# Expert jobs of a two-block transformer kernel: bias row a job ahead, scatter split in two, halves copied in another order

## Chip, cores and metric

The kernel runs on one core of a Trainium2 chip. The metric is the device time of one execution in microseconds; 2043.29 us is the median of three runs (2041.34 to 2046.06).

## The reference

A first block and a second block of two layers work on 256 tokens of width 1024, all in float32. The change touches one part of the first block: a mixture of 32 experts, of which each token uses 4.

```
def moe_ffn(h, w_router, b_router, w1, b1, w2, b2):
    logits = (hf @ w_router + b_router).astype(jnp.float32)
    top_val, top_idx = lax.top_k(logits, TOP_K)          # TOP_K = 4
    gates = jax.nn.softmax(top_val, axis=-1)
    ...
    def expert_block(args):
        xb, e = args
        hh = xb @ w1[e] + b1[e]                          # w1[e]: 1024 x 2048
        return swiglu_clamped(hh) @ w2[e] + b2[e]        # w2[e]: 1024 x 1024
```

The clamped SwiGLU takes the even columns of `hh` as `glu` (clamped above at 7) and the odd ones as `lin` (clamped to -7 .. 7) and gives `glu * sigmoid(1.702 * glu) * (lin + 1)`. The results are weighted with the gates and added up per token.

## The kernel before

A list of jobs is made on the chip once the router is done. A job is one expert with up to 64 of its tokens; an expert with more tokens gets a second job. Jobs are run two by two in a hardware loop on TensorE, ScalarE and VectorE each (`Fori(0, turns)`, r = 0 and 1 in each turn), and the engines meet only at semaphores.

Weights come through a ring of twelve buffers of 1 MB. SyncE issues the transfers (L405): an expert is twelve chunks, eight of w1 (chunks 0 to 7, one for each 128 rows) and four of w2 (8 to 11). Chunk j of the next expert may be issued when chunk j of the last job of the present expert has been used (`job_chunk`, counted up by TensorE behind each chunk).

One job on TensorE (`expert`, L800 to L842), in the order of its queue:

- w1 (L811): eight chunks, four matmuls each. The 64 tokens are the stationary operand; the two halves of the 2048 columns go to partitions 0 to 63 and 64 to 127 of banks 4 and 5.
- bias (L818): four matmuls with one row each, which add b1 as the last step of the sum; `hidden` tells VectorE.
- scatter (L792): eight matmuls that add the previous job's y, weighted with its gates, to the output in banks 0 to 3. It needs the previous y (L1382) and gate matrix (L1364).
- gather (L776): three of four blocks of tokens for the next pair of jobs; then the four transposes of the activation (L828), the last block of the gather, two transposes of gates (L782).
- w2 (L840): four chunks into bank 7, once ScalarE has copied the transposed activation (L1374).

In the profile each float32 matmul is two MATMUL instructions, so w1 has 64 of them, the bias 8, the scatter 16, w2 32.

VectorE in a job (L1843 to L1855): build index masks; wait for `hidden`; clamp glu (L1849) and lin (L1850) out of PSUM, each reading every second value of 1024; (lin + 1) * glu (L1853); wait for the sigmoid; the product (L1855), which is written in the order that the transposes want, as w2's rows lie in pairs: consecutive values go to places 128 values apart. ScalarE in a job (L1366 to L1382): issue the transfer of this job's b1 row (L1369), sigmoid (L1372), copy of the transposed activation (L1374), copies of gathered tokens and gates, copy of y (L1382).

"The middle" of a job below is the stretch from the last w1 matmul to the first w2 matmul.

Of the kernel before, what the change touches and what calls it, by code (L numbers as in the profile page):

```python
# [10 lines left out]
ALU = mybir.AluOpType  # L11
# [4 lines left out]
P = 128  # L16
D = 1024
T = 256
KT = D // P
# [15 lines left out]
E_N = 32  # L35
# [4 lines left out]
LISTED = 64  # L40
LIMIT = 7.0
# [15 lines left out]
CHUNK = 2048  # L57
N_ADA_A, N_WIN, N_ADA_B, N_WOUT = 8, 12, 16, 4
PER_EXPERT = 12
C_ADA_A = 0  # L60
C_WIN = C_ADA_A + N_ADA_A
C_ADA_B = C_WIN + N_WIN
# [111 lines left out]
sub_sq sub_ssq sub_root mix_ready dve_step   # L174
logits_ready top_ready e_ready masks_ready ranks_ready gates_ready gates_turned gates_saved tok_turned tok_saved
count_ready 
masks_built picks_built gathered half_saved xg_ready st_saved hidden hidden_read glu_ready sig_ready act_ready act_turned act_saved
y_saved pass_over b1_even b1_odd jobs_listed jobs_turned
moe_step job_chunk
rot_ready ret_v_ready ret_scores ret_weighted ret_out ret_sq ret_ssq ret_root  # L180
# [21 lines left out]
def two_layer_program(nc, x, c, w_ada, b_ada, g_pre_mix, g_post_mix, w_in, w_out, lam_q1, lam_k1, lam_q2,  # L202
# [4 lines left out]
    with ExitStack() as ctx:  # L207
# [3 lines left out]
        S = namedtuple("Semaphores", NAMES)(*[ctx.enter_context(nc.semaphore(n)) for n in NAMES])  # L211
# [11 lines left out]
        jobs = sbuf("jobs", 2 * LISTED + 2 + E_N, I32, rows=1)  # L223
        psum = ctx.enter_context(nc.psum_tensor("psum", [P, 8 * 512], F32))
        bank = [psum[:, 512 * i:512 * i + 512] for i in range(8)]
# [59 lines left out]
        pick = region(4608, TT * 2 * SLOTS).rearrange("p (a s) -> p a s", a=TT)  # L285
        pick_g = [region(4864 + 256 * i, TT * 2 * SLOTS).rearrange("p (a s) -> p a s", a=TT) for i in range(2)]
        glu, lin, sig, act_rows = (region(5376 + 512 * i, 512) for i in range(4))
        hidden_pairs = [t.rearrange("p (q m k) -> p q m k", q=2, k=2) for t in (lin, sig)]
        act_pairs = act_rows.rearrange("p (q k m) -> p q m k", q=2, k=2)
        b1_rows = [v[:, 0:1024].rearrange("p (h n) -> p h n", h=2) for v in (mixT, sq)]  # L290
        pos = region(15140, TT * (PASSES * E_N + 2)).rearrange("p (a e) -> p a e", a=TT)
        gate = region(9028, TT * 34).rearrange("p (a e) -> p a e", a=TT)
# [189 lines left out]
        def _(pe):  # L482
# [263 lines left out]
            for q in range(4):  # L746
                mm = routed_part(q)
# [34 lines left out]
                    mm = nc.tensor.transpose(home[:, a * P:(a + 1) * P], pick_g[r][:, a, :], ident)  # L782
                mm.then_inc(S.gathered, 1)

            def scatter(r, before, last=False):

                pe.wait_ge(S.y_saved, before + 1)
                pe.wait_ge(S.st_saved, before + 1)
                for t in range(4):
                    for h in range(2):  # L790
                        k, half = 4 * h + t, slice(64 * h, 64 * h + 64)
                        mm = nc.tensor.matmul(bank[k // 2][:, (k % 2) * T:(k % 2 + 1) * T],  # L792
                                              y_sb[half, t * P:(t + 1) * P], st_sb[r][half, :], start=False, stop=last,
                                              skip_group_check=True)
                return mm
# [4 lines left out]
            def expert(pair, r):  # L800
                e = pair * 2 + r
                weights = pe.value_load(jobs[0:1, bass.ds(pair * 2 + (LISTED + r), 1)], min_val=0, max_val=E_N - 1)
                if r == 0:
                    pe.wait_ge(S.xg_ready, pair + 1)
                pe.wait_ge(S.hidden_read, e + 1)
                pe.wait_ge(S.st_saved, e + 1)
                for k in range(KT):
                    chunk_here(weights, k)
                    for q in range(2):
                        for h in range(2):  # L810
                            mm = nc.tensor.matmul(bank[4 + q][64 * h:64 * h + 64, :], xg[:, k, SLOTS * r:SLOTS * (r + 1)],  # L811
                                                  ring[(C_MOE + k) % RING][:, (2 * h + q) * 512:(2 * h + q + 1) * 512],
                                                  start=(k == 0), stop=False)
                    mm.then_inc(S.job_chunk, 1)
                pe.wait_ge((S.b1_even, S.b1_odd)[r], pair * 16 + 16)
                for q in range(2):
                    for h in range(2):
                        mm = nc.tensor.matmul(bank[4 + q][64 * h:64 * h + 64, :], ones[64 * q:64 * q + 1, 0:64],  # L818
                                              b1_rows[r][64 * q:64 * q + 1, h, :], start=False, stop=True)
                mm.then_inc(S.hidden, 1)  # L820
                scatter(1 - r, e)
                if r == 0:
                    pe.wait_ge(S.picks_built, pair + 2)
                pe.wait_ge(S.half_saved, e + 2)
                gather(range(4 * r, 4 * r + 3), bank[6])
                pe.wait_ge(S.act_ready, e + 1)
                for t in range(4):
                    mm = nc.tensor.transpose(bank[4][:, t * P:(t + 1) * P], act_rows[:, t * P:(t + 1) * P], ident)  # L828
                mm.then_inc(S.act_turned, 1)
                gather((4 * r + 3,), bank[6])  # L830
                turn_gates(1 - r, e + 2, bank[5])
                pe.wait_ge(S.act_saved, e + 1)
                for j in range(8, 12):
                    chunk_here(weights, j)
                    w = ring[(C_MOE + j) % RING][:, :].rearrange("p (k n) -> p k n", k=2)
                    for k in range(2):
                        f = 2 * (j - 8) + k
                        at = (f % 4) * P + (f // 4) * 64
                        for h in range(2):
                            mm = nc.tensor.matmul(bank[7][64 * h:64 * h + 64, :], act_T[:, at:at + 64],  # L840
                                                  w[:, k, 512 * h:512 * h + 512], start=(f == 0), stop=(f == 7))
                    mm.then_inc(S.job_chunk, 1)  # L842
# [400 lines left out]
        def _(act):  # L1243
# [25 lines left out]
            at = KT  # L1269
# [95 lines left out]

            def expert(pair, r):  # L1366
                e = pair * 2 + r
                weights = act.value_load(jobs[0:1, bass.ds(pair * 2 + (LISTED + r), 1)], min_val=0, max_val=E_N - 1)
                act.dma_start(b1_rows[r][0:P:64], b1[0][bass.ds(weights, 1), :].rearrange("a (h q n) -> (a q) h n", h=2, q=2)) \  # L1369
                   .then_inc((S.b1_even, S.b1_odd)[r], 16)  # L1370
                act.wait_ge(S.glu_ready, e + 1)
                nc.scalar.activation(sig, glu, ACT.Sigmoid, scale=ALPHA).then_inc(S.sig_ready, 1)  # L1372
                act.wait_ge(S.act_turned, e + 1)
                nc.scalar.activation(act_T, bank[4], ACT.Copy).then_inc(S.act_saved, 1)  # L1374
                act.wait_ge(S.gathered, e + 2)
                save_half(r, bank[6], (xg_stage, xg[:, 4:8, :])[r])
                save_gates(1 - r, bank[5])
                if r == 1:
                    act.wait_ge(S.half_saved, e + 3)
                    nc.scalar.activation(xg[:, 0:4, :], xg_stage, ACT.Copy).then_inc(S.xg_ready, 1)  # L1380
                act.wait_ge(S.job_chunk, e * PER_EXPERT + PER_EXPERT)
                nc.scalar.activation(y_sb, bank[7], ACT.Copy).then_inc(S.y_saved, 1)  # L1382

            nc.scalar.activation(spare[:, 0:1], eps6, ACT.Copy).then_inc(S.y_saved, 1)
            act.wait_ge(S.count_ready, 1)
            turns = act.value_load(jobs[0:1, 2 * LISTED:2 * LISTED + 1], min_val=E_N // 2, max_val=E_N // 2 + 8)
            act.wait_ge(S.gathered, 1)
# [4 lines left out]
            with act.Fori(0, turns) as i:  # L1392
                for r in range(2):
                    expert(i, r)
            act.wait_ge(S.pass_over, 1)
            for q in range(4):
                square(psum, q)
# [196 lines left out]
        def _(dve):  # L1594
# [243 lines left out]
            with dve.Fori(0, turns) as i:  # L1838
                moe_chain.turn = i * 2
                for r in range(2):  # L1840
                    e = i * 2 + r

                    if r == 0:  # L1843
                        dve.wait_ge(S.gathered, e + 1)
                        pick_pair(lambda n: place_at(i * 2 + (n + 2)))
                    pick_gates(1 - r, place_at(i * 2 + (r + 1)), column_at(i * 2 + (r + 1)))
                    dve.wait_ge(S.hidden, e + 1)
                    both = psum[:, 4 * 512:6 * 512].rearrange("p (f g) -> p f g", g=2)
                    V.tensor_scalar(glu, both[:, :, 0], LIMIT, None, ALU.min).then_inc(S.glu_ready, 1)  # L1849
                    V.tensor_scalar(lin, both[:, :, 1], LIMIT, -LIMIT, ALU.min, ALU.max).then_inc(S.hidden_read, 1)  # L1850
                    dve.wait_ge(S.glu_ready, e + 1)
                    dve.wait_ge(S.hidden_read, e + 2)
                    moe_chain.link(V.scalar_tensor_tensor(out=lin, in0=lin, scalar=1.0, in1=glu, op0=ALU.add, op1=ALU.mult))  # L1853
                    dve.wait_ge(S.sig_ready, e + 1)
                    V.tensor_tensor(act_pairs, hidden_pairs[0], hidden_pairs[1], ALU.mult).then_inc(S.act_ready, 1)  # L1855
            onto_x(3, psum, 8, lambda q: only_gained(q, 88, gained_4))
            inverse(4)
            gained(88)
# [264 lines left out]
```

## Time and profile before

| | |
|---|---|
| median of 3 runs | 2043.29 us (2041.34 to 2046.06) |
| profiled execution | span 2042.2 us; the page gives no other time for it |
| TensorE busy | 1971.6 us (97%) |
| VectorE, ScalarE busy | 457.9 us (22%), 332.7 us (16%) |
| DMA | 562.30 MB, mean 275 GB/s; the expert weights are 384 transfers of 1 MB |
| chain that ended last | PE 79%, DMA 14%, SyncE's queue 4% |
| w1 matmuls (L811) | 2176 instructions, 491.0 us busy; 39.9 us idle ahead of them, nearly all for transfers |
| expert loop | first w1 matmul at 245.25 us, last y copy ends at 1207.4 us |

The page divides the span into 40 slices of 51 us. A matmul's duration is from its start to its modelled end, and matmuls overlap, so the time that one adds is read from the distance between starts.

### The profile page before, as it was taken

The numbers are of one execution on the slowest core, as the hardware profiler recorded it, in microseconds if no ns is written. First come the engines' busy times: TensorE is split into PE (matmuls) and PEld (weight loads), VectorE is DVE, ScalarE is ACT, GpSimd is POOL, SyncE is SP. The second block draws the span as 40 slices with busy tenths as digits, with TensorE's granted clock in tenths as the row PEclk, the third lists the DMA queues.
The fourth block names the chain that finished last, engine by engine and source line by source line (L and its number), as shares of the span: only waits on it lengthen the run. The fifth ranks groups of instructions, "written<-read, shape, count | busy, mean of one in ns | idle before, by whom it ended". The sixth has DMA issues, their size and how long they took to land.

```text
span 2042.2 us, 25651 instructions
## 1 busy us (share of the span) xinstructions
PE 1971.6 (97%) x10181; PEld 1262.8 (62%) x10182; DVE 457.9 (22%) x877; ACT 332.7 (16%) x689; POOL 19.1 (1%) x33
## 2 busy tenths in 40 slices
PE   7999999999999999999999989999999999999998
PEld 4876644433334444443333338788888899888887
DVE  1441311110111111111101122541010377410102
ACT  1232211111111111111111123431000121210001
POOL 2000000000000000000000000000000000000000
PEclk8999799999999999999999999999999999999999
DMA  9839299999999979999999996234445433344410
GB/s 350 284 120 405 85 422 421 422 422 422 421 383 373 422 314 421 422 421 421 422 421 422 422 367 202 92 124 141 148 149 160 140 108 104 124 144 153 157 42 21
DMA packets 170137, 562.30 MB, mean 275 GB/s; under 512 B 10486, under 2 KB 110104, under 8 KB 117600
## 3 DMA queue, kind: packets, MB, share of 16 engines
q1 hardware_dynamic: 167648, 554.96, 69.9%
q0 software_dynamic: 1664, 5.77, 1.0%
q8 instruction: 45, 0.74, 0.1%
q10 hardware_dynamic: 768, 0.74, 0.1%
q14 instruction: 12, 0.10, 0.0%
HBM read 560.38 MB, written 1.05 MB: 275 GB/s over the span
## 4 chain that ended last, share of the span: by engine, by line
PE 79%; DMA 14%; SPq 4%; DVE 1%; issue 1%; ACT 0%; DVEq 0%
PE psum L1106 15%; PE psum L811 14%; DMA ring<-in_w_dram 13%; PE psum L840 8%; PE psum L1078 7%; PE psum L1139 5%; PE psum L885 5%; SPq L405 4%; PE psum L654 4%; PE psum L570 3%; PE psum L776 3%; PE psum L792 2%; PE psum L1160 1%; PE psum L818 1%; PE psum L547 1%; DMA ring<-in_w_ada_dram 1%
## 5 line engine op out<-in xcount | busy, mean ns | idle before, releaser
L811 PE MATMUL psum<-ring,arena 128*64 128x512 f32 x2176 | 491.0, 596 | 39.9 <-DMA ring<-in_w_dram 39.7
L811 PEld LDWEIGHTS psum<-ring,arena 128*64 128x64 f32 x2176 | 152.3, 137 | 372.8 <-issue 252.9
L1106 PE MATMUL psum<-hT,ring 128*128 128x256 f32 x1408 | 307.5, 379 | 0.0
L1106 PEld LDWEIGHTS psum<-hT,ring 128*128 128x128 f32 x1408 | 267.5, 190 | 36.4
L840 PE MATMUL psum<-ring,arena 128*64 128x512 f32 x1088 | 241.0, 595 | 3.3
L1849 DVE TENSOR_SCALAR arena<-psum 128x512 f32<-128x512 f32 x34 | 23.5, 692 | 734.7 <-PE psum L818 734.7
L840 PEld LDWEIGHTS psum<-ring,arena 128*64 128x64 f32 x1088 | 77.7, 137 | 144.8 <-issue 144.8
L1078 PE MATMUL psum<-arena,ring 128*128 128x256 f32 x640 | 141.4, 379 | 0.0
L1078 PEld LDWEIGHTS psum<-arena,ring 128*128 128x128 f32 x640 | 121.6, 190 | 16.5
L1372 ACT ACTIVATE arena<-arena 128x512 f32<-128x512 f32 x34 | 21.4, 630 | 513.3 <-DVE arena L1849 513.3
L776 PE MATMUL psum<-arena 128*128 128x128 f32 x576 | 81.7, 288 | 0.0
L776 PEld LDWEIGHTS psum<-arena 128*128 128x128 f32 x576 | 72.2, 198 | 11.9 <-issue 11.9
L1139 PE MATMUL psum<-hT,ring 128*128 128x256 f32 x352 | 79.1, 379 | 0.0
L1534 ACT ACTIVATE arena<-arena 128x512 f32<-128x512 f32 x22 | 13.8, 629 | 394.5 <-DVE arena L1990 394.5
L792 PEld LDWEIGHTS psum<-arena 64*128 64x128 f32 x560 | 51.2, 186 | 33.8 <-issue 27.6
L1139 PEld LDWEIGHTS psum<-hT,ring 128*128 128x128 f32 x352 | 65.8, 190 | 10.1 <-issue 1.9
L792 PE MATMUL psum<-arena 64*128 64x256 f32 x560 | 69.9, 389 | 0.7 <-ACT arena L1382 0.7
L1990 DVE TENSOR_TENSOR arena<-psum,rstd 128x512 f32<-128x512 f32 x22 | 15.2, 692 | 238.3 <-PE psum L1106 238.3
L885 PE MATMUL psum<-hT,ring 128*128 128x256 f32 x288 | 66.3, 384 | 0.0
L570 PE MATMUL psum<-mixT,ring 128*128 128x256 f32 x288 | 63.9, 380 | 0.0
L654 PE MATMUL psum<-hT,ring 128*128 128x256 f32 x256 | 60.6, 394 | 0.5 <-DVE hT L1664 0.5
L885 PEld LDWEIGHTS psum<-hT,ring 128*128 128x128 f32 x288 | 53.8, 191 | 9.3 <-issue 2.4
(357 smaller groups left out, 1627.9 us busy)
## 6 DMA issues: line engine op xcount, KB each, us to landing
ring<-in_w_dram SPq DMA_DIRECT2D x384, 1024.0 KB, 22.8
ring<-in_ffn_w_dram SPq DMA_DIRECT2D x66, 1024.0 KB, 5.1
ring<-in_w_ada_dram SPq DMA_DIRECT2D x24, 1024.0 KB, 11.0
ring<-in_odd_w_in_dram SPq DMA_DIRECT2D x16, 1024.0 KB, 5.5
ring<-in_even_w_in_dram SPq DMA_DIRECT2D x13, 1024.0 KB, 12.7
ring<-in_w_in_dram SPq DMA_DIRECT2D x12, 1024.0 KB, 15.5
ring<-in_w_out_dram SPq DMA_DIRECT2D x4, 1024.0 KB, 15.6
ring<-in_even_w_out_dram SPq DMA_DIRECT2D x4, 1024.0 KB, 5.2
```

Source lines behind the costliest of these rows:

```text
L405: sp.dma_start(home[:, :], src).then_inc(landed[(C_MOE + j) % RING], 16)
L570: mm = nc.tensor.matmul(home[:, at:at + n_out], lhs, rhs, start=(k == 0), stop=(k == KT - 1))
L654: mm = nc.tensor.matmul(home, lhs, rhs, start=(k == 0), stop=(k == KT - 1))
L776: nc.tensor.matmul(home[:, (k % 4) * P:(k % 4 + 1) * P], h_tok[:, a, k * P:(k + 1) * P], pick[:, a, :], start=(a == 0), stop=(a == TT - 1))
L792: mm = nc.tensor.matmul(bank[k // 2][:, (k % 2) * T:(k % 2 + 1) * T], y_sb[half, t * P:(t + 1) * P], st_sb[r][half, :], start=False, stop= ...
L811: mm = nc.tensor.matmul(bank[4 + q][64 * h:64 * h + 64, :], xg[:, k, SLOTS * r:SLOTS * (r + 1)], ring[(C_MOE + k) % RING][:, (2 * h + q) * ...
L840: mm = nc.tensor.matmul(bank[7][64 * h:64 * h + 64, :], act_T[:, at:at + 64], w[:, k, 512 * h:512 * h + 512], start=(f == 0), stop=(f == 7))
L885: mm = nc.tensor.matmul(home[:, at:at + n_out], lhs, rhs, start=(k == 0), stop=(k == KT - 1))
L1078: mm = nc.tensor.matmul(bank[j // 2][:, (j % 2) * T:(j % 2 + 1) * T], w[:, k, j * P:(j + 1) * P], ffn_h[i % 2][:, k, :], start=(i == 0 and ...
L1106: mm = nc.tensor.matmul(bank[4 + 2 * (i % 2) + b][:, h * T:(h + 1) * T], cols(n)[:, k, h * P:(h + 1) * P], hT[:, k * T:(k + 1) * T], start ...
L1139: mm = nc.tensor.matmul(home, lhs, rhs, start=(k == 0), stop=(k == KT - 1))
L1849: V.tensor_scalar(glu, both[:, :, 0], LIMIT, None, ALU.min).then_inc(S.glu_ready, 1)
```

## The change

- **Bias.** ScalarE issues the transfer of the b1 row one job ahead (`load_b1` for the other buffer), and once ahead of the loop for expert 0. TensorE waits for the row and runs the four bias matmuls before w1, with `start=True`; the last w1 chunk ends the sum. The semaphore `hidden` is gone, VectorE waits for the eighth chunk of the job instead. Behind the loop ScalarE waits for the one row that was fetched in vain.
- **Scatter.** Its first half (t = 0, 1) runs behind w1's chunk 4 (k == SCATTER_AFTER), its second half (t = 2, 3) behind chunk 7, where all of it was.
- **Halves.** VectorE reads glu and lin with a step of four values, 256 of one parity and then 256 of the other, so that its results already lie in transposing order, and the product is written in order. The place of each block in the transposed activation changes with it (`at`).

```
-            def scatter(r, before, last=False):
+            def scatter(r, before, parts=range(4), last=False):
...
-                for t in range(4):
+                for t in parts:
...
+                pe.wait_ge((S.b1_even, S.b1_odd)[r], pair * 16 + 16)
+                for q in range(2):
+                    for h in range(2):
+                        nc.tensor.matmul(bank[4 + q][64 * h:64 * h + 64, :], ones[64 * q:64 * q + 1, 0:64],
+                                         b1_rows[r][64 * q:64 * q + 1, h, :], start=True, stop=False)
                 for k in range(KT):
                     chunk_here(weights, k)
...
-                                                  start=(k == 0), stop=False)
+                                                  start=False, stop=(k == KT - 1))
                     mm.then_inc(S.job_chunk, 1)
-                pe.wait_ge((S.b1_even, S.b1_odd)[r], pair * 16 + 16)
-                for q in range(2):
-                    for h in range(2):
-                        mm = nc.tensor.matmul(bank[4 + q][64 * h:64 * h + 64, :], ones[64 * q:64 * q + 1, 0:64],
-                                              b1_rows[r][64 * q:64 * q + 1, h, :], start=False, stop=True)
-                mm.then_inc(S.hidden, 1)
-                scatter(1 - r, e)
+                    if k == SCATTER_AFTER:
+                        scatter(1 - r, e, range(2))
+                scatter(1 - r, e, range(2, 4))
...
-                        at = (f % 4) * P + (f // 4) * 64
+                        at = (2 * k + j % 2) * P + (f // 4) * 64
...
-                weights = act.value_load(jobs[0:1, bass.ds(pair * 2 + (LISTED + r), 1)], min_val=0, max_val=E_N - 1)
-                act.dma_start(b1_rows[r][0:P:64], b1[0][bass.ds(weights, 1), :].rearrange("a (h q n) -> (a q) h n", h=2, q=2)) \
-                   .then_inc((S.b1_even, S.b1_odd)[r], 16)
+                following = act.value_load(jobs[0:1, bass.ds(pair * 2 + (LISTED + r + 1), 1)], min_val=0, max_val=E_N - 1)
+                load_b1(1 - r, b1[0][bass.ds(following, 1), :])
...
+            load_b1(0, b1[0][0:1, :])
             act.wait_ge(S.count_ready, 1)
...
+            act.wait_ge(S.b1_even, turns * 16 + 16)
             act.wait_ge(S.pass_over, 1)
...
-                    dve.wait_ge(S.hidden, e + 1)
-                    both = psum[:, 4 * 512:6 * 512].rearrange("p (f g) -> p f g", g=2)
-                    V.tensor_scalar(glu, both[:, :, 0], LIMIT, None, ALU.min).then_inc(S.glu_ready, 1)
-                    V.tensor_scalar(lin, both[:, :, 1], LIMIT, -LIMIT, ALU.min, ALU.max).then_inc(S.hidden_read, 1)
+                    dve.wait_ge(S.job_chunk, e * PER_EXPERT + KT)
+                    V.tensor_scalar(glu_rows, hidden_rows[:, 0], LIMIT, None, ALU.min).then_inc(S.glu_ready, 1)
+                    V.tensor_scalar(lin_rows, hidden_rows[:, 1], LIMIT, -LIMIT, ALU.min, ALU.max).then_inc(S.hidden_read, 1)
...
-                    V.tensor_tensor(act_pairs, hidden_pairs[0], hidden_pairs[1], ALU.mult).then_inc(S.act_ready, 1)
+                    V.tensor_tensor(act_rows, lin, sig, ALU.mult).then_inc(S.act_ready, 1)
```

with `hidden_rows = psum[:, 2048:3072].rearrange("p (n k g) -> p g k n", k=2, g=2)` and `glu_rows`, `lin_rows` the two buffers as `"p (k n) -> p k n"`.

## Rows read from the trace of the kernel before

**Rows 1.** The page's slices, line of GB/s moved by the DMA engines.
```profile
GB/s 350 284 120 405 85 422 421 422 422 422 421 383 373 422 314 421 422 421 421 422 421 422 422 367 202 92 124 141 148 149 160 140 108 104 124 144 153 157 42 21
```

**Rows 2.** Chain that ended last, 560 to 640 us: start us, us, what.
```profile
572.16 27.84 DMA ring<-in_w_dram
600.04 1.94 PE psum L811 x8
```

**Rows 3.** Timeline of VectorE, L1849: start us, us, engine, what [idle before <- releaser].
```profile
423.69 0.69 DVE L1849 TENSOR_SCALAR arena<-psum 128x512 f32<-128x512 f32 x1 [21.06 <-PE psum L818]
453.51 0.69 DVE L1849 TENSOR_SCALAR arena<-psum 128x512 f32<-128x512 f32 x1 [25.57 <-PE psum L818]
...
603.07 0.69 DVE L1849 TENSOR_SCALAR arena<-psum 128x512 f32<-128x512 f32 x1 [21.23 <-PE psum L818]
629.64 0.69 DVE L1849 TENSOR_SCALAR arena<-psum 128x512 f32<-128x512 f32 x1 [22.33 <-PE psum L818]
```

**Rows 4.** Windows: length, busy us by engine, clock, DMA share, GB/s.
```profile
609.00:616.00 7.00, 7.00 (x36) 2.44 (x34) 0.00 (x0) 0.69 (x2) 0.00 (x0) 1.00 0.01 2
...
739.00:750.00 11.00, 10.90 (x57) 4.54 (x58) 1.55 (x7) 3.13 (x8) 0.00 (x0) 1.00 0.01 3
```

**Rows 5.** Timeline, SyncE's queue, at the loop's start and behind both pauses.
```profile
247.38 12.33 SPq L405 DMA_DIRECT2D ring<-in_w_dram  x8
...
616.73 0.34 SPq L405 DMA_DIRECT2D ring<-in_w_dram  x1
...
749.58 0.34 SPq L405 DMA_DIRECT2D ring<-in_w_dram  x1
```

**Rows 6.** Timeline of one job, TensorE, VectorE and ScalarE.
```profile
641.22 13.91 PE L811 MATMUL psum<-ring,arena 128*64 128x512 f32 x64
641.43 0.60 ACT L1382 ACTIVATE arena<-psum 128x512 f32<-128x512 f32 x1 [5.25 <-PE psum L840]
642.70 1.01 ACTq L1369 DMA_DIRECT2D mixT<-in_b_dram  x1
...
655.06 1.09 PE L818 MATMUL psum<-mixT,early_sb 1*64 1x512 f32 x8
656.07 2.00 PE L792 MATMUL psum<-arena 64*128 64x256 f32 x16
656.21 0.69 DVE L1849 TENSOR_SCALAR arena<-psum 128x512 f32<-128x512 f32 x1 [17.80 <-PE psum L818]
...
658.00 1.60 PE L776 MATMUL psum<-arena 128*128 128x128 f32 x12
658.33 1.07 DVE L1855 TENSOR_TENSOR arena<-arena 128x512 f32<-128x512 f32 x1
...
660.87 7.09 PE L840 MATMUL psum<-ring,arena 128*64 128x512 f32 x32
```

**Rows 7.** Timeline, TensorE's weight loads, same job.
```profile
655.05 0.21 PEld L818 LDWEIGHTS psum<-mixT,early_sb 1*64 1x64 f32 x8 [0.81 <-issue]
656.07 1.60 PEld L792 LDWEIGHTS psum<-arena 64*128 64x128 f32 x16 [0.81 <-issue]
...
667.36 0.15 PEld L811 LDWEIGHTS psum<-ring,arena 128*64 128x64 f32 x2 [0.28 <-issue]
```

**Rows 8.** Groups by line and form, VectorE: count, busy us, mean ns, idle before.
```profile
L1855 DVE TENSOR_TENSOR arena<-arena 128x512 f32<-128x512 f32 x34 | 36.5, 1072 | 1.2
...
L1849 DVE TENSOR_SCALAR arena<-psum 128x512 f32<-128x512 f32 x34 | 23.5, 692 | 734.7 <-PE psum L818 734.7
...
L1994 DVE TENSOR_TENSOR arena<-arena 128x512 f32<-128x512 f32 x22 | 15.2, 692 | 0.7
...
L1990 DVE TENSOR_TENSOR arena<-psum,rstd 128x512 f32<-128x512 f32 x22 | 15.2, 692 | 238.3 <-PE psum L1106 238.3
```

**Rows 9.** Timeline, the next stage's first transfers and its first matmul.
```profile
1178.89 46.49 SPq L375 DMA_DIRECT2D ring<-in_even_w_in_dram  x10
...
1218.35 1.10 PE L885 MATMUL psum<-arena,ring 128*128 128x256 f32 x4 [0.18 <-DVE arena L1605]
```

More of the change, by code:

```diff
@@ L59 @@
 PER_EXPERT = 12
+SCATTER_AFTER = 4
 C_ADA_A = 0
@@ L176 @@
 count_ready
-masks_built picks_built gathered half_saved xg_ready st_saved hidden hidden_read glu_ready sig_ready act_ready act_turned act_saved
+masks_built picks_built gathered half_saved xg_ready st_saved hidden_read glu_ready sig_ready act_ready act_turned act_saved
 y_saved pass_over b1_even b1_odd jobs_listed jobs_turned
@@ L287, in two_layer_program @@
         glu, lin, sig, act_rows = (region(5376 + 512 * i, 512) for i in range(4))
-        hidden_pairs = [t.rearrange("p (q m k) -> p q m k", q=2, k=2) for t in (lin, sig)]
-        act_pairs = act_rows.rearrange("p (q k m) -> p q m k", q=2, k=2)
+        hidden_rows = psum[:, 2048:3072].rearrange("p (n k g) -> p g k n", k=2, g=2)
+        glu_rows, lin_rows = (t.rearrange("p (k n) -> p k n", k=2) for t in (glu, lin))
         b1_rows = [v[:, 0:1024].rearrange("p (h n) -> p h n", h=2) for v in (mixT, sq)]
@@ L1382, in expert, with load_b1 @@
                 nc.scalar.activation(y_sb, bank[7], ACT.Copy).then_inc(S.y_saved, 1)
+            def load_b1(r, row):
+                act.dma_start(b1_rows[r][0:P:64], row.rearrange("a (h q n) -> (a q) h n", h=2, q=2)) \
+                   .then_inc((S.b1_even, S.b1_odd)[r], 16)
             nc.scalar.activation(spare[:, 0:1], eps6, ACT.Copy).then_inc(S.y_saved, 1)
+            load_b1(0, b1[0][0:1, :])
             act.wait_ge(S.count_ready, 1)
```

## The prediction

> **What bounds the kernel now.** I read the slices first [rows 1]. TensorE is busy nearly everywhere (97% of the span by the page), but from the sixth slice to the twenty-third, the expert loop, the rate of the DMA engines is flat, 421 or 422 GB/s in all but three. There are two full resources, and busy shares don't say which one counts. The chain of waits [rows 2] says which of the two ends last. Up to 600.04 us it is the weight transfer, and each new expert costs twelve chunks of it: VectorE's first read of a job comes 29.82 us after the one before (423.69, 453.51), 2.49 us a chunk [rows 3]. From 600.04 us it is TensorE alone, and the same mark comes every 26.57 us (603.07, 629.64). So a job is worth 26.6 us of TensorE or 29.8 us of transfer.
>
> Why do the two change places? 34 jobs (L1849's count, [rows 8]) serve 32 experts. An expert with a second job keeps its twelve chunks in the ring, and SyncE can fetch nothing until the second job frees them. In 609 to 616 and in 739 to 750 us the DMA share is 0.01 [rows 4], and the next transfers are issued at 616.73 and 749.58 us [rows 5], when the second job has finished its first chunk. The same happens at the start of the loop: the first new transfer goes out at 247.38 us, once the first job has done one chunk. After each restart the transfers run without a hole, so every microsecond by which a restart comes later stays in the loop, until something after the last transfer gives it back. The path is therefore:
> (a) first job's start to its first chunk's end (TensorE), then transfers until the chunk w1-7 of the job that reads at 603.07;
> (b) from there TensorE: the middle of that job, its w2, and the first chunk of the next job (616.73);
> (c) 616.73 to 749.58 = 132.85 us = 5 periods of 26.57, TensorE;
> (d) transfers again until w1-7 of the last job;
> (e) TensorE: middle and w2 of the last job, and all that follows.
> On this path there are therefore seven middles (one in b, five in c, one in e), seven job starts (a, b, five in c) and five passes over chunks 4 and 5 of w1 (c). In the other jobs the transfers run without a hole beside TensorE; where it waits for them it has 29.82 - 26.57 = 3.25 us of cover a job.
>
> **The change, part by part.** One TensorE-bound job is in [rows 6]. It starts at 641.22, the next one 26.57 later, at 667.79. Its w1 is 64 instructions, two every 0.429 us (its weight loads: 0.15 us and 0.28 idle, [rows 7]), so 32 x 0.429 = 13.73 us, to 654.95. The middle goes from there to 660.87, 5.92 us, and w2 takes the last 6.92.
>
> *The middle, g.* Now: bias from 655.06, VectorE starts at 656.21 (0.06 after the modelled end of the bias, 656.15), ends the product at 658.33 + 1.07 = 659.40, w2 starts at 660.87. TensorE is not idle there: scatter 656.07 to 658.00, so 0.121 us for each of its sixteen, then the gather's twelve at the same pace, 1.45 us, to 659.45. Both engines are ready for the transposes at the same moment, so speeding up one of them alone would bring nothing. After: VectorE waits for w1-7 itself, whose matmuls end at 641.22 + 13.91 = 655.13, so it starts at about 655.19, 1.02 us earlier. Its product writes in order instead of by a step of 128 values: 1072 ns (L1855, [rows 8]) becomes the 692 ns of the same form at L1994, 0.38 less. TensorE's own queue then has half the scatter, 0.97, and the gather, 1.45: ready 2.4 us after the last chunk, VectorE after 0.24 + (659.40 - 656.21) - 0.38 = 3.05. VectorE is last, and the middle is 5.92 - 1.02 - 0.38 = 4.52. g = -1.40 us. What is late next: TensorE now idles 0.6 us in the hole that the scatter used to fill.
>
> *The bias at the start, b.* Its eight instructions are not gone, they stand before w1. The boundary between w2 and the next w1 has no gap today (L811's weight loads follow L840's with the usual 0.28 us idle, [rows 7]), so they are paid in full: 655.06 to 656.07 is 1.01 us, and 0.11 for the change of shape ahead of it: b = +1.12. Bounds: 0.86 from two slots of 0.43 us with nothing for the changes of shape, 1.15 with one more 0.14. The prefetch itself costs nothing: the same one 8 KB issue a job on ScalarE's queue (1.0 us, at its old place behind the y copy [rows 6]), needed 26 us later instead of 13; one more issue stands before the loop, where ScalarE only waits for the router. ScalarE's new wait behind the loop is for a transfer issued at the last job's start, some 30 us before.
>
> *Half of the scatter after chunk 4, s.* Eight of sixteen instructions leave the middle (counted above) and stand in a w1 that had no hole in (c). 1.93 us / 2 = 0.97, and again entering and leaving another shape: s = +1.12; bounds 0.86 (four slots of half of 0.43) and 1.25. Its waits are met: y is saved at 641.43 + 0.60 = 642.03, the scatter would be asked for at about 651. What is queued behind it, chunks 5 to 7, shifts by s.
>
> *Reading the halves from PSUM.* VectorE takes every fourth value instead of every second. Bounds: 692 as now, or the 1072 of L1855, whose stepping is the only slow one in the loop. I take 692: the step of two already costs no more than the step of one (L1849 against L1990, both 692, [rows 8]). The higher end is a rival.
>
> A change of shape shows in TensorE's weight loads: inside w1 they stand idle for 0.28 us between pairs, before the bias and before the scatter for 0.81 [rows 7], as none is loaded ahead there. The old order has four such changes a job, the new one seven. Without them b and s would be at their low bounds, which is rival 2. A rule of the Trainium skill stands behind this, and it speaks against the inserted pieces: by "TensorEngine Tiling (Array Packing)", Key Properties, another tiling mode, unlike another tile of the same mode, makes TensorE drain first. The trace agrees.
>
> **The sum.** 7b + 5s + 7g = 7.84 + 5.60 - 9.80 = **+3.6 us**. In steps: restart (a) +1.12; (b) -1.40 + 1.12, so +0.84 at the first pause's end; (c) five periods of 26.57 + 0.84 = 27.41, so +5.04 at the second; (d) nothing, because 27.41 is still under 29.82; (e) -1.40. Behind the loop TensorE goes on as before: at 1218.35 it starts on the next stage's first chunk after 0.18 us of waiting for VectorE, and that stage's chunks are issued from 1178.89 on [rows 9], so the shift is carried to the end. Why a shorter middle doesn't pay: only seven of 34 lie on the path, and there TensorE was full already, so what leaves the middle is paid elsewhere.
> With b and s low, g as it is: 6.02 + 4.30 - 9.80 = +0.5. With both high and g = -1.35: 8.05 + 6.25 - 9.45 = +4.9. The profiled span is 2042.2 us (the page gives no other time for it), which makes 2045.8; the median of the three runs is 2043.29, 1.1 higher, and 2046.9 on that footing. The runs spread over 4.7 us.
>
> **Rivals.**
> 1. *The wide step in PSUM is slow.* Both reads at L1849 and L1850 cost 0.38 more, in a row, before the third operation; g = -1.40 + 0.76 = -0.64, the period 28.2. Time: 7.84 + 5.60 - 4.48 = +9.0, 2052.3 us. It decides as soon as the two reads are over 750 ns. For it: L1855 shows that a step can cost half as much again. Against it: 692 at step two. The Trainium skill, "SBUF — State Buffer", Specifications (TRN2), has a rule that points to this rival: PSUM is read in lines of 8 bytes, and each access that crosses into a new line pays. By that rule the step of two, where each value lies in a line of its own, would pay already, and the row shows that it does not; for step four no run here has a number.
> 2. *Inserted work slips in cheaply.* The bias and the half scatter use parts of the array side by side, and if the changes of shape cost nothing at their new places we are at +0.5: 2043.8 us. For it: the pieces are short. Against: idle weight loads at each such change.
> 3. *The product stays slow*, because its two inputs and not its output pattern make 1072 ns. Then g = -1.02 and the sum is +6.3: 2049.6. Against it: L1994 has two inputs in SBUF as well and takes 692.
> 4. *Faster.* Bias, scatter and gather fill the middle up to 659.45, and of the 1.42 us behind that at most 0.4 is a wait for ScalarE's copy of the activation (an estimate, from 0.60 for the y copy of the same size less what is queued beside it). Even a perfect filling gives five times 0.4 and 1.4 at the tail, -3.4: 2039.9. Nothing in the diff takes work off TensorE.
>
> **Chances.** Forecast 0.70 with its own range 2044 to 2049; rival 1 0.12; rival 2 0.10; rival 3 0.04; rival 4 0.04. What can be told from no change is about 0.2%, 4.1 us, and the forecast stands just inside: of its 0.70 I put 0.27 above the line, 0.42 within, 0.01 below. Slower 0.27 + 0.12 + 0.04 = 0.43; same 0.42 + 0.10 = 0.52; faster 0.05. The range of eight in ten goes from the low end of rival 2 less a microsecond of spread, 2042.7, to 2051, which leaves out most of rival 1.
>
> **What the changed profile would show.** The VectorE mark every 27.4 us between the two pauses (it was 26.57), 29.8 to 30.0 elsewhere. DMA restarts later than before against the first job's start by 1.1, 0.8 and 5.0 us. From the last w1 matmul's issue to w2 4.5 us. L1855's successor at 692 ns, the two reads at 692. TensorE's weight loads idle before and after the inserted half scatter. From the last job's w1-7 to the end 1.4 us less. The stretch bound by TensorE after the second pause lasts longer, since only 2.4 us instead of 3.3 of the lead are used up in each job. I am wrong if the period is under 26.6 (then b or s is hidden), if it is over 28 (the reads), or if the time moves outside the expert loop.

## The result, and the profile after

| | before | changed |
|---|---|---|
| median of 20 runs each | 2042.33 us (2039.03 to 2046.52) | 2045.53 us (2042.89 to 2050.67) |
| ratio | | 1.0020, 95% interval 1.0014 to 1.0026: +2.9 to +5.3 us |
| span of the profiled run | 2042.2 us | 2042.7 us |
| period between the two pauses | 26.57 us | 27.54 us |
| first job's start to the first matmul of the next stage | 973.10 us | 978.64 us |

The forecast was +3.6 us. The change costs about 0.2%; the interval starts at 0.14%, so it is clear of no change. The two spans differ by only 0.5 us because the profiled run of the changed kernel reached its first job 4.8 us earlier (240.42 against 245.25). That moment wanders: over the traces of all kernels below it lies between 240.4 and 245.5 us, and for the changed kernel itself at 240.42 and 243.36. So from here on traces are compared from the first job's start. Its first matmul and the next stage's first (as [rows 9]) are:

```profile
240.42 1.09 PE L811 MATMUL psum<-mixT,early_sb 1*64 1x512 f32 x8 [0.16 <-issue]
...
1219.06 1.10 PE L887 MATMUL psum<-arena,ring 128*128 128x256 f32 x4 [0.18 <-DVE arena L1612]
```

The wait of 0.18 us in front of the next stage is the one of before; all that was lost was lost in the loop.

The timeline of VectorE, first read of a job (as [rows 3]), in the changed kernel:

```profile
599.32 0.69 DVE L1855 TENSOR_SCALAR arena<-psum 128x512 f32<-128x512 f32 x1 [21.64 <-PE psum L817]
626.86 0.69 DVE L1855 TENSOR_SCALAR arena<-psum 128x512 f32<-128x512 f32 x1 [23.30 <-PE psum L817]
```

27.54 us where it was 26.57. The timeline of a job (as [rows 6]; its w1 began at 666.71 - 27.54 = 639.17) shows of what this is made:

```profile
647.91 1.13 PE L793 MATMUL psum<-arena 64*128 64x256 f32 x8
648.97 5.37 PE L817 MATMUL psum<-ring,arena 128*64 128x512 f32 x24
654.27 1.13 PE L793 MATMUL psum<-arena 64*128 64x256 f32 x8
654.39 0.69 DVE L1855 TENSOR_SCALAR arena<-psum 128x512 f32<-128x512 f32 x1 [19.14 <-PE psum L817]
...
655.34 1.60 PE L777 MATMUL psum<-arena 128*128 128x128 f32 x12
...
656.51 0.69 DVE L1861 TENSOR_TENSOR arena<-arena 128x512 f32<-128x512 f32 x1
657.25 0.66 PE L830 MATMUL psum<-early_sb,arena 128*128 128x128 f32 x4 [0.31 <-DVE arena L1861]
...
658.67 7.09 PE L842 MATMUL psum<-ring,arena 128*64 128x512 f32 x32
...
665.69 1.09 PE L811 MATMUL psum<-sq,early_sb 1*64 1x512 f32 x8
666.71 5.80 PE L817 MATMUL psum<-ring,arena 128*64 128x512 f32 x26
```

Five chunks take 8.58 us and end at 647.75; w1 goes on at 648.97, so s = 1.22. The other three end at 654.12, w2 starts at 658.67: the middle is 4.55, g = -1.37. The rest of 27.54 (less 13.73 of w1 and 6.92 of w2) is b = 1.12. TensorE now waits for VectorE in the middle: 0.31 us at the transposes (L830), where it never did. VectorE's groups (as [rows 8]):

```profile
L1861 DVE TENSOR_TENSOR arena<-arena 128x512 f32<-128x512 f32 x34 | 23.5, 691 | 1.2
L1855 DVE TENSOR_SCALAR arena<-psum 128x512 f32<-128x512 f32 x34 | 23.5, 691 | 746.6 <-PE psum L817 746.6
```

The product fell from 1072 to 691 ns, and the read with a step of four costs no more than with a step of two. Weight loads around the inserted half (as [rows 7]):

```profile
646.95 0.14 PEld L817 LDWEIGHTS psum<-ring,arena 128*64 128x64 f32 x2 [0.28 <-issue]
647.91 0.73 PEld L793 LDWEIGHTS psum<-arena 64*128 64x128 f32 x8 [0.81 <-issue]
648.97 0.20 PEld L817 LDWEIGHTS psum<-ring,arena 128*64 128x64 f32 x4 [0.33 <-issue]
```

Ahead of the inserted half the loads stand idle for 0.81 us, as before every change of shape in [rows 7]. Behind it, back in w1, it is 0.33 instead of the usual 0.28.

SyncE's restarts of the transfers (as [rows 5]):

```profile
243.57 0.34 SPq L406 DMA_DIRECT2D ring<-in_w_dram  x1
...
613.77 0.34 SPq L406 DMA_DIRECT2D ring<-in_w_dram  x1
...
751.45 0.34 SPq L406 DMA_DIRECT2D ring<-in_w_dram  x1
```

Against the first job's start these are 3.15, 373.35 and 511.03 us. Before they were 2.13, 371.48 and 504.33. So the restarts come +1.0, +1.9 and +6.7 us later, where +1.1, +0.8 and +5.0 were forecast.

### The profile page after: what moved, and what is told of

It reads as the page before. It is cut to its first block, busy times and chain, and to the rows that moved or that the text cites. A ratio compares the mean times of both kernels' runs of the same rounds, so it can differ in the third digit from the quotient of the medians.

```text
span 2042.7 us, 25722 instructions
## 1 busy us (share of the span) xinstructions
PE 1983.2 (97%) x10181; PEld 1251.0 (61%) x10182; DVE 444.8 (22%) x877; ACT 332.5 (16%) x689; POOL 19.0 (1%) x33
## 4 chain that ended last, share of the span: by engine, by line
PE 77%; DMA 14%; DVE 4%; SPq 3%; issue 1%; ACT 0%; DVEq 0%; ACTq 0%
PE psum L817 15%; PE psum L1108 15%; DMA ring<-in_w_dram 13%; PE psum L842 8%; PE psum L1080 7%; PE psum L1141 5%; PE psum L887 5%; PE psum L655 4%; PE psum L571 3%; SPq L406 3%; PE psum L1162 1%; PE psum L793 1%; DMA ring<-in_w_ada_dram 1%; PE psum L811 1%; PE psum L548 1%
## 5 line engine op out<-in xcount | busy, mean ns | idle before, releaser
L817 PEld LDWEIGHTS psum<-ring,arena 128*64 128x64 f32 x2176 | 145.6, 136 | 346.0 <-issue 277.2
L842 PEld LDWEIGHTS psum<-ring,arena 128*64 128x64 f32 x1088 | 77.7, 137 | 144.7 <-issue 144.7
L793 PE MATMUL psum<-arena 64*128 64x256 f32 x560 | 79.1, 402 | 0.7 <-ACT arena L1383 0.7
```

## The experiments

"Marks" are from the trace: the period between the pauses, and N, the time from the first job's start to the first matmul of the next stage. The kernel before has N = 973.10 and, in a second trace (b0), 973.62; differences are against their mean, 973.36. A ratio is against runs of the kernel before on the same chip. The sum column is 7b + 5s + 7g with each kernel's own b, s and g (in e7 two of the seven b leave the path). The marks come from one trace each, the times from 4 to 20 runs. In nine of the thirteen rows the time lies under the marks, in one by 2.7 us, in others up to 0.9 us above; I can't explain this, and differences of a microsecond or two between rows should not be read.

| kernel | period | N, diff. | sum | ratio and interval | as us |
|---|---|---|---|---|---|
| changed | 27.54 | +5.3 | +4.4 | 1.0020 (1.0014 to 1.0026) | +4.1 |
| a0 changed, again | 27.54 | +5.2 | +4.4 | 1.0019 (1.0007 to 1.0030) | +3.9 |
| b0 before, again | 26.57 | +0.3 | 0 | 1.0006 (0.9994 to 1.0017) | +1.2 |
| e1 bias first only | 26.71 | +1.0 | +1.0 | 0.9995 (0.9985 to 1.0006) | -1.0 |
| e2 whole scatter in the middle | 26.65 | 0.0 | +0.6 | 0.9993 (0.9984 to 1.0002) | -1.4 |
| e3 bias last | 27.41 | +6.8 | +3.4 | 1.0036 (1.0022 to 1.0049) | +7.4 |
| e3b bias last, again | 27.41 | +7.2 | +3.4 | 1.0031 (1.0022 to 1.0040) | +6.3 |
| e4 order only | 26.50 | -1.0 | -0.5 | 0.9997 (0.9987 to 1.0007) | -0.6 |
| e5 inserted half in two pieces | 27.89 | +7.4 | +6.1 | 1.0026 (1.0016 to 1.0037) | +5.3 |
| e6 bias twice | 28.40 | +10.5 | +10.4 | 1.0050 (1.0035 to 1.0065) | +10.2 |
| e7 bias behind chunk 0 | 26.65 | +0.2 | -1.7 | 0.9988 (0.9978 to 0.9997) | -2.5 |
| e8 whole scatter behind chunk 4 | 28.40 | +11.3 | +8.7 | 1.0056 (1.0041 to 1.0072) | +11.4 |
| e9 whole scatter ahead of w1 | 28.25 | +12.0 | +11.8 | 1.0052 (1.0032 to 1.0072) | +10.6 |

**Which part costs: e1, e2, e3, e4.** Each kernel has some of the three parts.

e1, from the changed kernel, and the halves as before (`both`, `act_pairs`, `f % 4`):

```
-                    if k == SCATTER_AFTER:
-                        scatter(1 - r, e, range(2))
-                scatter(1 - r, e, range(2, 4))
+                scatter(1 - r, e)
```

> The changed kernel with the whole scatter back in the middle and the halves in the old order, so only the bias moved. Path theory (7b + 5s + 7g, with the prices that the changed kernel's trace shows: b 1.12, s 1.22): the middle is then bound by TensorE's scatter and gather, about 4.95 us, g = -0.97; period between the pauses 26.72 us; sum 7 x 0.15 = +1.0 us over the kernel before, which can't be told from no change. Rival (the chain of VectorE alone sets the middle): g = -1.02, much the same here; it parts from the first in e2. Rival (a shorter middle pays in every job): -33 us.

e2: the same edit, the halves in the new order.

> The changed kernel with the whole scatter back in the middle, all else as changed. Path theory: TensorE binds the middle at 4.95 us although VectorE's product is 0.38 shorter, period 26.72, +1.0 us over the kernel before and 3.3 us less than the changed kernel. Rival (VectorE's chain sets the middle): 4.55 us, period 26.32, 7b + 7g = -1.8 us. Rival (the loss of the changed kernel is not the half scatter): as the changed kernel, +3 to +4 us, period 27.5.

Measured: neither can be told from the kernel before, and both lie under the changed kernel; the periods are 26.71 and 26.65, where 26.72 was expected of both. e2's middle:

```profile
654.55 2.00 PE L793 MATMUL psum<-arena 64*128 64x256 f32 x16
654.67 0.69 DVE L1853 TENSOR_SCALAR arena<-psum 128x512 f32<-128x512 f32 x1 [17.93 <-PE psum L817]
...
656.48 1.60 PE L777 MATMUL psum<-arena 128*128 128x128 f32 x12
656.79 0.69 DVE L1859 TENSOR_TENSOR arena<-arena 128x512 f32<-128x512 f32 x1
657.92 0.60 PE L828 MATMUL psum<-early_sb,arena 128*128 128x128 f32 x4
```

VectorE's product ends at 657.48, but the transposes start at 657.92 and wait for nobody: TensorE's own scatter and gather fill the time. Bias first takes 1.0 us out of the middle and puts it in front of w1; nothing is won or lost. The half scatter is what turns this into a loss.

e3, from the kernel before, with the new order of halves:

```
                     mm.then_inc(S.job_chunk, 1)
+                    if k == 4:
+                        scatter(1 - r, e, range(2))
...
-                scatter(1 - r, e)
+                scatter(1 - r, e, range(2, 4))
```

> The kernel before with the scatter split (half behind chunk 4) and the halves in the new order; the bias stays last. Path theory: middle 5.92 - 0.38 = 5.54 us, period 26.57 + 1.22 - 0.38 = 27.41, sum 5 x 1.22 - 7 x 0.38 = +3.4 us over the kernel before. Rival (bias first is what costs): +0, period 26.6. Rival (the inserted half costs only its share of the columns, 0.86): period 27.05, +1.6 us.

The period was as expected, 27.41, but time and marks were twice the sum. I measured it again:

> The kernel before with split scatter and new order, bias last, measured again, because its first time (+7 us, interval 4.5 to 10) lay over the +3.4 of the sum. If the excess was in the transfers' own pace (the first trace had 30.0 us an expert from its first marks), this time comes nearer to +3.4 and the trace shows 29.8 for longer; if it belongs to this order of work, +7 again. Period 27.41 either way.

It was +6.3 again, with 29.6 to 30.0 us an expert at VectorE from the first marks on that the transfers set. The excess belongs to this order of work; below.

e4, from the kernel before: only the three lines of VectorE, the two views and `at` of the change.

> The kernel before with the halves in the new order only. Path theory: the product takes 692 ns instead of 1072, but TensorE is busy with scatter and gather until the same moment as before, so the middle stays at 5.9 us, the period at 26.57 and the time within 0.1% of the kernel before. Rival (VectorE's chain sets the middle): middle 5.54, period 26.19, -2.7 us.

Measured: as expected; 26.50 against 26.57. A product shorter by 0.38 us brought 0.07, as TensorE was not waiting for it.

**What an inserted piece costs: e5, e6, e8.**

e5, from the changed kernel:

```
-                    if k == SCATTER_AFTER:
-                        scatter(1 - r, e, range(2))
+                    if k in (2, 5):
+                        scatter(1 - r, e, (k // 3,))
```

> The changed kernel with the half scatter inside w1 in two pieces: t = 0 behind chunk 2, t = 1 behind chunk 5. Same instructions, two more changes of shape in a job. If a pair of changes costs 0.37 us (1.22 less 0.85 of columns): s = 1.59, period 27.9 us against 27.54, +1.9 us over the changed kernel, +5 to +6 over the kernel before. Rival (changes of shape are free, the eight instructions themselves take 1.2): period 27.5, no difference from the changed kernel.

Its timeline in w1:

```profile
643.72 5.37 PE L817 MATMUL psum<-ring,arena 128*64 128x512 f32 x24
649.02 0.70 PE L793 MATMUL psum<-arena 64*128 64x256 f32 x4
649.65 5.37 PE L817 MATMUL psum<-ring,arena 128*64 128x512 f32 x24
```

Three chunks end at 643.72 + 5.15 = 648.87 and w1 goes on at 649.65: 0.78 us for four instructions, where eight cost 1.22. The period grew by 0.35 us with the same instructions, so an excursion out of w1's shape and back costs 0.35 by itself. That is shown. What in the excursion costs it is not taken apart: the second piece also brings two more semaphore waits, both long met. They are the less likely cause, as w1 has such a wait ahead of each of its chunks and keeps its 0.43 us a pair.

In the marks e5 lies 1.3 us over its sum. The hole in the transfers told of below comes to as much, 0.3 us behind the first and 1.0 us behind the third restart.

e6, from the changed kernel: the four bias matmuls stand there twice, the second time with `start=False`; this kernel adds the bias twice.

> The changed kernel with the four bias matmuls issued twice, so that the bias is added twice. b grows by about 0.86 us without another change of shape. Path theory (seven job starts count): period 28.4 us, 7 x 0.86 = +6.0 over the changed kernel, some +10 over the kernel before. Rival (all 34 jobs are on the path): +29 over the changed kernel. Rival (transfers hide all of it): no difference from the changed kernel.

Measured: 28.40 and +10.2. This is the test of the path: 0.86 us more in each of 34 jobs moved the end by 10.5 - 5.3 = 5.2 us in the marks, near 7 x 0.86 = 6.0 and far from 29. The missing 0.8 is the part of the changed kernel's +5.3 that its own sum, +4.4, does not cover. e6 has no such excess (+10.5, sum +10.4), and the hole in the transfers, told of below, is not in its trace.

e8, from the changed kernel: `scatter(1 - r, e)` behind chunk 4, nothing behind chunk 7.

> The changed kernel with the whole scatter behind chunk 4, none in the middle. Path theory: the middle stays at 4.55 us, as VectorE's chain binds it already; s = 2.1 us, period 28.4, 7b + 5s + 7g = +8.7 us over the kernel before. Rival (what leaves the middle is gained there): middle 3.5, period 27.4, as the changed kernel.

Measured: period 28.40 as the path theory had it. The middle did not shrink when the second half left it.

**The excess: e3, a0, b0, e9.** e3 came out at twice its sum, and e8 2.6 us above. A hole is here a stretch in which the transfers move less than their usual 422 GB/s. In e3 I looked at windows behind the restarts (columns as [rows 4]), 20 to 24 and 24 to 28 us after 244.24 and 752.47:

```profile
264.24:268.24 4.00, 4.00 (x20) 1.34 (x18) 0.00 (x0) 0.00 (x0) 0.00 (x0) 1.00 0.94 346
268.24:272.24 4.00, 4.00 (x22) 1.42 (x20) 0.00 (x0) 0.60 (x1) 0.00 (x0) 1.00 0.98 320
772.47:776.47 4.00, 4.00 (x20) 1.34 (x18) 0.00 (x0) 0.00 (x0) 0.00 (x0) 1.00 0.92 328
776.47:780.47 4.00, 4.00 (x22) 1.44 (x20) 0.00 (x0) 0.60 (x1) 0.00 (x0) 1.00 0.96 311
```

and the same in the kernel before, behind 247.38:

```profile
267.38:271.38 4.00, 4.00 (x20) 1.34 (x18) 0.00 (x0) 0.00 (x0) 0.00 (x0) 1.00 1.01 424
271.38:275.38 4.00, 4.00 (x22) 1.42 (x20) 0.00 (x0) 0.60 (x1) 0.00 (x0) 1.00 1.02 424
```

At 422 GB/s the first pair of e3's windows lacks (76 + 102) x 4 / 422 = 1.7 us of transfer, the second 1.9 us; the kernel before lacks nothing there. In e3's second trace (e3b) the same windows lack 1.4 and 1.9 us. This is where the transfers come to the end of the eight chunks that w1 freed, and the ninth (the first of w2) is freed only after the middle. SyncE issues that ninth transfer in e3 at 264.77, 20.53 us behind the restart; in the kernel before at 267.06, 19.68 behind it; in the changed kernel at 263.05, 19.48:

```profile
264.77 0.33 SPq L405 DMA_DIRECT2D ring<-in_w_dram  x1
```

e8 has 20.35 us and lacks 1.4 to 1.7 us at each restart. e5 has 19.83 and lacks 0.3, 1.0 and 1.0, here at its third restart (757.40):

```profile
777.40:781.40 4.00, 4.00 (x22) 1.40 (x20) 0.00 (x0) 0.00 (x0) 0.00 (x0) 1.00 0.94 371
781.40:785.40 4.00, 4.00 (x24) 1.03 (x22) 0.00 (x0) 0.60 (x1) 0.00 (x0) 1.00 0.93 365
```

The changed kernel lies on the edge: 0.5 + 0.5 us at its first restart,

```profile
263.57:267.57 4.00, 4.00 (x22) 1.34 (x18) 0.00 (x0) 0.00 (x0) 0.00 (x0) 1.00 1.03 367
267.57:271.57 4.00, 4.00 (x24) 1.12 (x22) 0.00 (x0) 0.60 (x1) 0.00 (x0) 1.00 0.96 373
```

and nothing there in a second trace:

> The changed kernel once more, for a second trace. Where transfers set the time, the first trace has a new expert every 29.8 us up to 479 us and every 30.0 us after it; the kernel before has 29.8 up to 543. If that point wanders from run to run by itself, it lies elsewhere in this trace and the pause ends up to 1 us earlier or later against the first job's start; if the inserted scatter brings it forward, it lies where it was. The period between the pauses stays 27.54 either way.

> The kernel before once more, for a second trace. Period between the pauses 26.57 us. If the step from 29.8 to 30.0 us an expert wanders by itself, it lies elsewhere than at 543 us; if it belongs to the kernel, there.

Measured: the pace of 29.8 us an expert lasted to the first pause in a0, but in b0 only for two intervals (30.0 from the mark at 452.75 us on, in the first trace from 543.05). So that step wanders by itself, 0.17 us an expert, and the hole is a matter of its own. e9 tests the account of the hole: the whole scatter between bias and w1, thus ahead of the restart.

```
+                scatter(1 - r, e)
                 for k in range(KT):
...
-                    if k == SCATTER_AFTER:
-                        scatter(1 - r, e, range(2))
-                scatter(1 - r, e, range(2, 4))
```

> As the kernel with the whole scatter behind chunk 4 (e8), but the scatter stands between bias and w1. New theory: where chunk 8 is freed 20.3 us or more behind a restart of the transfers (20.4 in e8), the transfers run short for a moment, 1.4 to 1.7 us of transfer in the 8 us from 20 to 28 us behind each restart. Here the scatter is ahead of the restart, chunk 8 is freed 18.3 us behind it, and that loss should fall to under 0.2 us at all three restarts; the period stays 28.4 us; the restarts come 2.1 us later after the first job's start than in e8 at the loop's start. Sum 7 (b + s + g) = +12.8 us without holes, against +8.4 plus two holes of 1.5 in e8. Rival (the shortage comes from inserted work as such or from traffic on ScalarE's queue): loss of 1.4 to 1.7 us at each restart as in e8, and +16 us.

Its windows 20 to 28 us behind the first and third restart:

```profile
266.93:270.93 4.00, 4.00 (x24) 1.10 (x20) 0.00 (x0) 0.60 (x1) 0.00 (x0) 1.00 1.01 422
270.93:274.93 4.00, 4.00 (x30) 2.20 (x28) 0.00 (x0) 0.00 (x0) 0.00 (x0) 1.00 1.01 420
...
779.73:783.73 4.00, 4.00 (x24) 1.10 (x20) 0.00 (x0) 0.60 (x1) 0.00 (x0) 1.00 1.00 416
783.73:787.73 4.00, 4.00 (x30) 2.21 (x28) 0.00 (x0) 0.00 (x0) 0.00 (x0) 1.00 1.02 424
```

No hole (ninth transfer 18.27 us behind the restart), and N is +12.0 where the sum says +11.8. A period of 28.25 instead of the 28.4 I wrote makes the sum; the scatter next to the bias has one change of shape less.

e9 leaves a rival, though. Its ninth transfer is issued earlier, and at the same time nothing is inserted behind the restart any more, so chunks 5 to 7 come free earlier too. The holes of 0.5 us and more all stand in kernels with work inserted in w1. Against that rival speak the kernels that have none there, but a ninth transfer at 19.6 to 19.8 us: behind the second restart it landed 4.48 us (kernel before), 3.78 (e4) and 4.91 us (e7) after the eighth, where 2.49 is usual, though the bytes moved there lack only 0.3 to 0.4 us. With a ninth at 18.3 to 18.7 (e1, e2, e9) it landed on time at all nine restarts. A longer middle without inserted work would decide it and was not run.

**Bias behind the first chunk: e7.** From the changed kernel with the whole scatter in the middle: the wait for the row and the four bias matmuls (`start=False`) stand behind chunk 0, whose first matmul opens the sum.

> The changed kernel with the whole scatter in the middle and the bias behind chunk 0 instead of ahead of it. The first chunk is freed without the bias at the loop's start and after both pauses, so two of seven b leave the path: 5b + 7g = 5.6 - 6.8 = -1.2 us against the kernel before, period 26.72, restart of the transfers 2.1 us after the first job's start instead of 3.15. Rival (position makes no difference): +1.0, as e2.

Measured: ratio 0.9988, interval 0.9978 to 0.9997, against the kernel before, which just leaves out no change, and clearly under the changed kernel, whose interval starts at 1.0014. The restart is 243.68 - 241.55 = 2.13 us behind the first job's start, as foreseen. In the marks it is +0.2, not -1.7; the transfers lack 0.6 to 1.2 us between 4 and 12 us behind its restarts, where the kernel before lacks 0.1 to 0.6, and for which I have no experiment. That it is faster than the kernel before would rest on the times alone, and time and marks part by 2.7 us here, so I take it as not shown. Against e2, with the same middle and all seven b, e7's restarts behind the pauses come 1.26 us earlier (371.20 against 372.46, 504.45 against 505.71), so something of the two b did leave the path; it is lost again behind the last restart.

## Why the prediction was right

The path, the signs and the three prices held. One step, (d), was partly wrong, and its error adds to those of s and g. The steps in order, with what each measured:

- *Only seven middles of 34 count; a period is paid five times.* Shown by e6: doubling a term of every job moved the end by 5.2 us, six times its price (seven times, once the changed kernel's excess of 0.8 over its sum is taken off), and not 34 times. e1, e6 and e9 meet 7b + 5s + 7g within 0.3 us in the marks, e2 and e4 within 0.6. The changed kernel itself (0.8 and 0.9 over), e5 (1.3), e7 (1.9), e8 (2.6) and e3 (3.4 and 3.8) do not.
- *g = -1.40*: -1.37. VectorE's earlier finish alone was not enough; half of the scatter had to leave the middle too. e2 and e4 show it, where TensorE still is last, and so does the 0.31 us wait at L830. I had put TensorE's idle time at 0.6.
- *b = +1.12*: 1.12.
- *s = +1.12*: 1.22, of which 0.35 is for leaving w1's shape and coming back (e5). I had allowed 0.26, the 1.12 less the 0.86 of the low bound. This is worth 5 x 0.10 = 0.5 us.
- *(d) "transfers again", nothing lost behind a restart*: this step was not fully right. With scatter inserted in w1 (changed, e3, e5, e8) the transfers can have a hole 20 us behind a restart. It added up to 1 us in one trace of the changed kernel and none at that place in the other; in e3 it is 3.6 us on the path in the first trace and 3.3 in the second, of excesses of 3.4 and 3.8. The two traces have the restart behind the first pause 1.4 and 1.8 us late (373.00 and 373.35 against a mean of 371.58) instead of 0.8. In the second trace, without a hole, the windows from 4 to 8 us behind the first and third restart lack 1.2 and 0.8 us (before: 0.6 and 0.1); what is left I put down to the wandering pace, which no experiment controls.
- *The sum*: +3.6 forecast, +4.4 with the measured prices, +5.2 and +5.3 in the marks, +2.9 to +5.3 in the times. That the forecast is nearer to the time (+4.1) than to the marks is luck: the 1.2 us between the two is not explained.
- *Rival 1 (the wide step is slow)* fell: 691 ns at a step of four. The Trainium skill's rule of the 8-byte line in PSUM ("SBUF — State Buffer", Specifications (TRN2)) would have made both reads slower; for VectorE's float32 reads the traces show no such cost at steps of 8 ([rows 8]) and 16 bytes, so the measurement decides. *Rival 2 (cheap insertion)* fell with b = 1.12 and s = 1.22 against its 0.86, and with e5. *Rival 3* fell: 691 ns for the product. *Rival 4 (faster)* did not come.

The chances were nearly evenly put between "same" and "slower", parted at 0.2%, and the result stands on that line: 0.20%, interval 0.14 to 0.26.

## What to carry to other kernels

Where two resources take turns as the bound, find the stretches in which each lies on the path and count an edit's price once for each of them; a shorter chain behind a full engine wins nothing, and what is moved off it is paid where it lands. Work of another matmul shape should stand next to a change of shape that is there anyway, as each excursion cost about a third of a microsecond here. In a ring of buffers look also at the spacing with which buffers come free: work inserted ahead of the next release can starve the transfers although the mean rate would do.

## What the runs showed that I had not expected

- The transfers ran short 20 to 28 us behind every restart where the ninth transfer was issued late. Three restarts are in each trace; the loss is in us of transfer at 422 GB/s:

| ninth issued, us behind the restart | kernels | lost |
|---|---|---|
| 18.3 to 18.7 | e1, e2, e9 | none in nine restarts |
| 19.48 | changed, a0, e6 | 1.0 and 1.2 at two of nine, else up to 0.1 |
| 19.6 to 19.8 | before, b0, e4, e7 | up to 0.35 in twelve |
| 19.83 | e5 | 0.3, 1.0, 1.0 |
| 20.35 to 20.53 | e8, e3, e3b | 0.7 to 1.9 at all nine |

  The losses don't follow the spacing alone: the kernels of the second, fourth and fifth row have work inserted in w1, those of the third have none. The eighth transfer lands only 22 to 25 us behind the restart, so the ninth is issued while transfers are still under way, and yet there is a hole. Why, these traces don't show.
- The pace of the transfers has two values, 29.8 and 30.0 us for an expert of 12.6 MB. It passes from the first to the second at different places in two traces of the same kernel. By the landing times it mostly falls back behind a restart: in the kernel before, twelve transfers take 29.8 us again for the first four experts behind 749.58 us, then 30.0. Why, I can't say.
